# A decoder trunk's sparse-attention mixer: 24 index scores in four groups of six instead of six groups of four

## The reference, cut to what matters

```
q, c_kv, q_i, k_i, w_i, gate_b, x_b = split(h @ w_in, EVEN_SPLITS)
# sparse attention: per 128 queries, 8 index heads choose up to 128 keys
sc    = einsum('bqhd,bsd->bqhs', q_i, k_i) * 64 ** -0.5
score = einsum('bqhs,bqh->bqs', relu(sc), w_i * 8 ** -0.5)
score = where(causal, score, -inf);  idx = top_k(score, 128)
# softmax attention of 8 heads over the chosen keys, k and v from rmsnorm(c_kv)
# recurrent branch
xc    = causal_dwconv(x_b, conv_w, conv_b)          # 4 taps, 512 channels
b_out = rg_lru(xc, ...) * gelu(gate_b)
out   = concatenate([a_out, b_out]) @ w_out
```

## Time and profile before

| | |
|---|---|
| median of three runs | 2181.17 us |
| the profiled execution, its own time | 2181.75 us |
| its span, first to last instruction | 2180.0 us |
| busy in the span: PE, DVE, ACT, POOL | 99%, 67%, 52%, 5% |
| granted clock of PE over the span | 0.999 of full speed |
| chain that ended last, by engine | PE 91%, DVE 5%, ACT 2%, POOL 1%, DMA 1% |

### The profile page before, as it was taken

How to read it: one execution, slowest core, us unless ns; L and a number is a source line. 1 busy time by engine, 2 the same in 40 slices (tenths; PEclk the granted TensorE clock), 3 DMA queues, 4 the chain that set the end, 5 groups by cost and what they waited for, 6 DMA issues and landing times.

```text
span 2180.0 us, 36486 instructions
## 1 busy us (share of the span) xinstructions
PE 2163.3 (99%) x13768; PEld 1944.7 (89%) x13768; DVE 1453.7 (67%) x2179; ACT 1130.1 (52%) x1887; POOL 110.4 (5%) x104
## 2 busy tenths in 40 slices
PE   9999999999999999999999999999999999999998
PEld 8999888775888899998899998898889889999987
DVE  8888635798565688874388886354356567888732
ACT  6555534476554555554365555245445546555531
POOL 0000000576000000000000000000000000000000
PEclk9999999999999999999999999999999999999999
DMA  4332332221452233323323333323323422333332
GB/s 165 106 106 96 116 99 71 78 72 55 135 165 78 78 115 98 105 95 118 126 70 104 106 106 106 106 75 104 103 77 120 155 82 74 102 103 103 115 97 78
DMA packets 62017, 221.51 MB, mean 102 GB/s; under 512 B 7985, under 2 KB 8113, under 8 KB 61922
## 3 DMA queue, kind: packets, MB, share of 16 engines
q1 hardware_dynamic: 57456, 208.69, 29.4%
q10 hardware_dynamic: 4466, 11.53, 1.5%
HBM read 218.09 MB, written 2.10 MB: 101 GB/s over the span
## 4 chain that ended last, share of the span: by engine, by line
PE 91%; DVE 5%; ACT 2%; DMA 1%; POOL 1%; issue 1%; DVEq 0%; POOLq 0%; ACTq 0%
PE ps L2116 12%; PE ps L2118 12%; PE ps L2117 12%; PE ps L2212 11%; PE ps L2214 11%; PE ps L2213 11%; PE ps L481 6%; PE ps L482 5%; PE ps L483 5%; PE ps L2052 1%; DMA w_raw<-in_wstream 1%; DVE w_lo L419 1%; DVE e_sc L1776 1%; DVE e_max L1775 1%; DVE e_sc L1791 1%
## 5 line engine op out<-in xcount | busy, mean ns | idle before, releaser
L419 DVE TENSOR_TENSOR w_lo<-w_raw,w_hi 128x1024 fp32r<-128x1024 f32 x204 | 252.2, 1240 | 350.9 <-ACT w_hi L414 349.9
L414 ACT ACTIVATE w_hi<-w_raw 128x1024 fp32r<-128x1024 f32 x210 | 221.7, 1057 | 322.3 <-PE ps L2214 216.9
L2116 PE MATMUL ps<-t_hi,w_hi 128*128 128x256 f32 x1280 | 362.3, 283 | 0.0
L2118 PE MATMUL ps<-t_hi,w_lo 128*128 128x256 f32 x1280 | 362.3, 283 | 0.0
L2117 PE MATMUL ps<-t_lo,w_hi 128*128 128x256 f32 x1280 | 362.3, 283 | 0.0
L2118 PE MATMUL ps<-x_hi,w_lo 128*128 128x256 f32 x960 | 271.7, 283 | 0.0
L2117 PE MATMUL ps<-x_lo,w_hi 128*128 128x256 f32 x960 | 271.7, 283 | 0.0
L2116 PE MATMUL ps<-x_hi,w_hi 128*128 128x256 f32 x960 | 271.7, 283 | 0.0
L1498 DVE TENSOR_TENSOR w_lo<-f,w_hi 128x1024 fp32r<-128x1024 f32 x152 | 186.1, 1224 | 124.2 <-ACT w_hi L841 124.2
L481 PE MATMUL ps<-x_hi,w_hi 128*128 128x256 f32 (+1 forms) x736 | 250.7, 341 | 2.0 <-DVE x_lo L1375 1.0
L482 PE MATMUL ps<-x_lo,w_hi 128*128 128x256 f32 (+1 forms) x736 | 246.0, 334 | 0.0
(11 more groups left out here) (358 smaller groups left out, 4308.1 us busy)
## 6 DMA issues: line engine op xcount, KB each, us to landing
w_raw<-in_wstream SPq DMA_DIRECT2D x310, 512.0 KB, 3.7
w_raw_odd<-in_wstream SPq DMA_DIRECT2D x80, 512.0 KB, 3.6
tmp<-in_post_gains ACTq DMA_DIRECT2D x8, 512.0 KB, 4.5
gain_bc<-in_gains ACTq DMA_DIRECT2D x7, 512.0 KB, 3.8
h<-in_x SPq DMA_DIRECT2D x4, 512.0 KB, 6.2
c_mem<-in_mem ACTq DMA_DIRECT2D x2, 1024.0 KB, 5.5
out_dram<-h SPq DMA_DIRECT2D x3, 512.0 KB, 2.7
c_gain<-in_mem_gains ACTq DMA_DIRECT2D x2, 512.0 KB, 7.6
```

The lines of the kernel that those rows point to most:

```text
L414: nc.scalar.activation(weights(v)[0], raw(v), ACT.Copy).then_inc(w_hi_ready, 1)
L419: nc.vector.tensor_tensor(wl, raw(v), wh.bitcast(f32), ALU.subtract).then_inc(w_ready, 1)
L2116: nc.tensor.matmul(dst, wh[:, at], xh[:, b, :], start=first, stop=False, skip_group_check=True)
L2118: last = nc.tensor.matmul(dst, wl[:, at], xh[:, b, :], start=False, stop=final, skip_group_check=True)
```

## The change

The 24 scores go in four groups of six in place of six groups of four, and the blocks of x_b between them are dealt out anew. `done` still begins at 3 for the three blocks ahead of the transposes; the new table counts from there.

```
-        IN_FRONT = (6, 1, 5, 6, 6, 5)
+        IN_FRONT = (6, 5, 9, 9)
...
                 for n in range((TT - 1) * IH):
-                    if n % 4 == 0:
-                        blocks("x_b", done, sum(IN_FRONT[:n // 4 + 1]) - done)
-                        done = sum(IN_FRONT[:n // 4 + 1])
+                    if n % 6 == 0:
+                        blocks("x_b", done, 3 + sum(IN_FRONT[:n // 6 + 1]) - done)
+                        done = 3 + sum(IN_FRONT[:n // 6 + 1])
```

## The result

The changed kernel takes 2185.77 us (median of 12 runs, 2185.1 to 2187.91), the kernel before, run beside it on the same chip, 2181.43 (12 runs, 2180.52 to 2182.96): a ratio of 1.0021, 95% interval 1.0012 to 1.003, slower by 4.34 us. The profiled execution took 2185.59, its span is 2183.8, against 2181.75 and 2180.0.

The account below looks back on a forecast made before the run. PE is busy 99%, but DVE's parallel chain was already the later at L2439, so its 3.7 us lag sets the end: 2180.0 + 3.7 + 1.75 = 2185.45, less 0.58, gives 2184.9 us; range 2182.6 to 2187.0.

Parts of the forecast that it names:

- the favoured case: Whole kernel: DVE's lag of 3.3 to 4.3 us sets the end, 2184.4 to 2185.5 us; chance 0.56.
- the long half clock: Rival, in c_kv: half speed costs PE 3.4 us instead of 1.7, PE 5.3 late, 2186.5 us; chance 0.07.
- the sum: Whole kernel: span 2180.0 + 3.7 + 1.75 = 2185.45, less 0.58 to the median, 2184.9 us.
- Steps 1 to 5: First scores to q 0's lowering: scores 2.04 us later, DVE idle 1.8, its lag 4.6, 4.8, then 3.7.
- step 6: At score 22: PE stands some 2.7 us waiting for accumulations and is 2.75 us late in front of c_kv.
- Step 3's open case: Splitting c_kv 0: whether DVE's lowering waits for POOL's one-input operation; taken that it does, otherwise 0.4 us less.
- Step 5: Lowering of q 0: DVE waits only 0.10 us for POOL instead of 1.22, so its lag falls to 3.7.
- the missed gap: Rival, at q 0's lowering: DVE arrives 0.2 us later and meets POOL's next operation; lag 4.8, 2186.0 us; chance 0.24.
- It is covered, just: In c_kv: PE, losing 1.7 us to half clock, is 3.63 us late, still behind DVE's 3.7.
- step 7: At L2439: PE meets the chain from DVE over ACT, 3.7 us late; all engines then late by that.
- the last rival: Not slower: scores 6 and 7 come in time, 2180.2 us; the clock fall at 526 may go, 1.7 more; chance 0.06.

Follow-up runs that it names:

- e3: The changed kernel with twelve identity matmuls as filler in front of score 22, where PE stood idle; 2184.4 us, ratio 1.0014.
- e1: The kernel before, groups of four kept, with three x_b blocks moved from behind the scores to the front; 2184.62 us, ratio 1.0015.
- e6: The changed kernel, groups of six kept, with three x_b blocks moved from the front back behind the scores; 2183.83 us, ratio 1.0012.
- e5: e2 with three selection rounds moved from ahead of c_kv's mean square to behind c_kv's lower halves; 2185.71 us, ratio 1.0016.
- e7: The changed kernel with blocks dealt 6, 3, 9, 14 and one selection round moved behind c_kv's lower halves; 2184.56 us, ratio 1.0013.
- e2: The changed kernel with the last two x_b blocks and three c_kv blocks issued in front of score 22; 2186.25 us, ratio 1.0022.
- e4: The changed kernel with the four selection rounds behind score 15 moved behind score 23; 2188.14 us, ratio 1.0033.

## Why the prediction was right, and where it was not

The time and its sign came out (2184.9 forecast, 2185.77 measured; +3.7 forecast, +4.34 measured; a span of 2183.7 forecast, 2183.8 profiled). That it came so near is in part luck. The measured time lies just above the 2184.4 to 2185.5 of the favoured case, between it and the long half clock's 2186.5. Two misses of opposite sign made the span: the sum had the loss at gate 0.9 too small and did not count that part of such a loss comes back behind gate.

| Step | Forecast | After, by before's mark |
|---|---|---|
| 1. first score, score 6 | 399.81, 405.02 | 399.83, 404.95 |
| 2. DVE idle before accumulation 6 | 1.8 | 1.56 |
| 3. rounds start | 409.58 | 409.36 |
| 4. behind c_kv 1 | 416.54, 4.8 late | 416.30, 4.55 late |
| 5. lowering of q 0 waits; lag | 0.10; 3.7 | 0.08; 3.43 |
| 6. stand at score 22 | 2.7 | 2.15 |
| 6. PE late in front of c_kv | 2.75 | 3.31, part of it half clock |
| clock lost | 1.7 | 3.4 |
| 7. PE late at L2439 | 3.7, waiting 1.2 or next to nothing | 5.06, no wait |
| gate | 3.7 | 4.62 |

Steps 1 to 5 hold to 0.3 us (0.08 is 1.21 less the free 1.13). In step 6 the old start of c_kv, 426.08 by the sum, is 426.21 in the trace of before; the 3.31 counts from there. Step 3's open case is settled: DVE's lowering took 1.62 and its next operation came 0.99 behind the end of the one-input L595 (408.28). So it had waited for it, as before it waited for L600. The Trainium skill ("SBUF — State Buffer", SBUF: two separate sides) has VectorE's operations with two SBUF inputs locked out by any GpSimd operation that reads SBUF and started first. The trace agrees: 1.62 instead of 1.21. Step 5, the closest call, fell on the side that I took: the missed gap did not occur.

The step that failed is the clock, "It is covered, just", and with it step 7, where PE should have come to L2439 no later than DVE's lag. Half speed lasted from about 427 to 433.7 and cost 3.4 us instead of the 1.7 that I took from the one fall in the earlier trace rows. The rival "the half clock lasts twice as long" is what happened in c_kv: PE came 5.38 after its old arrival, 5.06 after its old start; the rival's 5.3 was close. I had given it 0.07. It moved the total by less than the rival said (4.62 at gate instead of 5.3), since ACT's wait for q 1, not L2439, passes it on. That the clock makes this part is shown by e3, where the same lag of DVE without the half clock gives 3.50 at gate.

DVE's lag is the root of it, but it acts in two ways, and the prediction had them the wrong way round. In after itself the way that binds is the one over PE: late accumulation 16, the stand, the half clock, ACT's wait for q 1. The way over the mean square and the root, on which the sum stood, is 1.16 us less late; e3 shows that it binds once the half clock is gone, at 3.50. e1 and e6 show where the lag at the mean square comes from: 2.10 of three more blocks in front, 1.41 of groups of six.

A third way was not in the prediction at all: e5 and e7 show a chain over POOL, a DMA and ACT. In after it lets ACT take the root at 451.60 (452.30 less 0.70), 2.8 late, so that it would have kept most of the loss even without DVE's lag at the mean square. I had counted POOL's work only where it meets DVE, and of the DMAs only that none changes its place in the order; the fetch of q 3 kept its place and came 3.4 us later (449.24 in after, 445.96 in before, at the upper half made from it). Nor did the sum count that the fall at 526 may go; only the last rival names it. Gate is 4.62 late, the profiled span only 3.8 longer; the half clock at 526, some 1.7 us in before and none in after, is the change that the rows show behind gate, though it is more than the difference.

## What to carry to other kernels

When an order moves a producer later, follow every engine that it releases to the next point where their chains meet, and count each lag there, DMAs and table loads included: taking away the visible wait may only show the next chain, as e5 did. Price a stand of PE as its length plus the half clock that may follow, with a range for the fall (here nothing to 3.4 us) and not the one value that the trace happens to show. When a wait is filled with useful work taken from later, ask what PE will lack there; e2 lost as much as the kernel that it was to mend.

## What the runs showed of the hardware

- The same stand, 2.15 us in front of score 22, was followed by 3.4 us of lost clock in after and by none in e6, with PE busy for 0.92 of the 3 us from 423.5 to 426.5 in after and for 0.89 of the 3 us from 422 to 425 in e6. The fall near 526 comes and goes as well: before, e1, e2 and e4 have one between 526 and 534, after and the other seven do not.
- Runs of one and the same kernel differ like this too. The granted clock over the span is 1.000 in the two fastest of e6's 11 runs (2182.67 and 2183.16 us, the second is the profiled one) and 0.997 in its two slowest (2186.48, 2187.17); in e2 it is 1.000 at 2183.73 and 2183.80 and 0.997 at 2189.42. So the order of the instructions does not settle by itself whether the clock falls; at which stand it fell in the runs without a trace is not known. The Trainium skill ("TensorE: Matmul & The Clock Gate", What's actually happening) says that the activity window of the clock gate is free-running and does not reset when a kernel starts, so that the number of slow matmuls at a kernel's start varies from run to run. It says so of the start and not of a stand in the middle; that the same holds here would fit, and is not shown.
- Waits of 2.36 to 5.91 us at L2439's matmul were followed by half clock in the profile of each of the five kernels that had one (e1, e2, e4, e5, e7; in e4 the fall began within the wait), and gate was later than the later of DVE and PE by 1.2 to 1.6 us in each.
- DVE's two-input lowering and POOL keep each other out in both directions, also for a one-input operation of POOL: the lowering behind L595 took 1.62 instead of 1.21, and POOL's L598 that met it took 1.88 instead of 1.04.
